# Down-projection of a hybrid decoder layer as seven products of halves, with its weight sums made during attention

## The reference, cut to what matters

```python
hn = rms_norm(h, ffn_norm_w[l])
up = causal_depthwise_conv(hn @ w_up[l], ffn_conv_w[l], ffn_conv_b[l])
a, gt = jnp.split(up, 2, axis=-1)
h = h + (jax.nn.silu(gt) * a) @ w_down[l]
```

## Time and profile before

| | |
|---|---|
| median of 3 runs | 1972.78 us (1972.56 to 1973.24) |
| profiled execution, its own time | 1971.36 us |
| its span | 1969.6 us |
| mean granted TensorE clock | 0.995 of full |
| matmuls | 9113 |
| PE busy | 97% of the span |

### The profile page before, as it was taken

One profiled execution on the slowest core, in us unless ns is written; L12 is line 12 of the kernel. 1 busy time (PEld: TensorE's weight loads), 2 busy tenths in 40 slices (PEclk: granted clock), 3 DMA queues, 4 the chain that ended last, 5 costly groups with the idle time before them and its releaser, 6 DMA issues. The chain is left out here.

```text
span 1969.6 us, 24174 instructions
## 1 busy us (share of the span) xinstructions
PE 1918.9 (97%) x9113; PEld 1646.5 (84%) x9113; DVE 1098.5 (56%) x1413; ACT 738.2 (37%) x1324; POOL 99.1 (5%) x153
## 2 busy tenths in 40 slices
PE   6999999999999998999999999989999999999999
PEld 5788999999998887787888887868888888878887
DVE  5535632453351776897425625478778787643433
ACT  6323532442243154312613322445544454432222
POOL 1101110111010010000100001000000000000000
PEclk9999999999999999999999999999999999999999
DMA  7211221021113101102113405113232232264312
GB/s 245 97 43 44 71 70 43 12 81 49 43 60 113 43 1 43 43 22 65 43 33 93 154 23 171 65 43 97 64 96 74 86 93 67 85 239 146 111 48 75
DMA packets 112412, 152.33 MB, mean 77 GB/s; under 512 B 13705, under 2 KB 60809, under 8 KB 112329
## 3 DMA queue, kind: packets, MB, share of 16 engines
q1 hardware_dynamic: 104265, 140.60, 22.0%
q10 hardware_dynamic: 8064, 10.59, 1.5%
HBM read 122.73 MB, written 28.43 MB: 77 GB/s over the span
## 5 line engine op out<-in xcount | busy, mean ns | idle before, releaser
L240 PE MATMUL psum<-whi,act_lo 128*128 128x512 f32 x768 | 314.9, 410 | 3.5 <-DVE act_lo L1431 2.9
L242 PE MATMUL psum<-whi,act_hi 128*128 128x512 f32 x768 | 304.4, 396 | 0.0
L241 PE MATMUL psum<-wlo,act_hi 128*128 128x512 f32 x768 | 304.4, 396 | 0.0
L240 PEld LDWEIGHTS psum<-whi,act_lo 128*128 128x128 f32 x768 | 194.9, 254 | 18.7 <-issue 4.5
L242 PEld LDWEIGHTS psum<-whi,act_hi 128*128 128x128 f32 x768 | 195.1, 254 | 15.3
L241 PEld LDWEIGHTS psum<-wlo,act_hi 128*128 128x128 f32 x768 | 196.0, 255 | 13.2
L240 PE MATMUL psum<-act_hi,wlo 128*128 128x512 f32 x512 | 202.2, 395 | 1.3 <-DVE wlo L198 1.3
L242 PE MATMUL psum<-act_hi,whi 128*128 128x512 f32 x512 | 199.6, 390 | 0.0
L241 PE MATMUL psum<-act_lo,whi 128*128 128x512 f32 x512 | 199.3, 389 | 0.0
L193 ACT CAST whi<-stage 128x512 fp32r<-128x512 f32 x200 | 120.3, 621 | 180.9 <-PE psum L242 172.6
L198 DVE TENSOR_TENSOR wlo<-stage,whi 128x512 fp32r<-128x512 f32 x200 | 129.0, 686 | 94.7 <-ACT whi L193 93.9
(11 more groups left out here) (248 smaller groups left out, 3572.5 us busy)
## 6 DMA issues: line engine op xcount, KB each, us to landing
stage<-in_w_in SPq DMA_DIRECT2D x144, 256.0 KB, 4.0
u_raw<-in_w_up SPq DMA_DIRECT2D x44, 512.0 KB, 5.0
gated_scratch<-g_buf SPq DMA_DIRECT2D x22, 512.0 KB, 2.7
gated<-gated_scratch SPq DMA_DIRECT2D x22, 512.0 KB, 3.5
d_stage<-in_w_down SPq DMA_DIRECT2D x44, 256.0 KB, 2.8
group_out<-ob ACTq DMA_DIRECT2D x24, 256.0 KB, 2.1
grp<-group_out SPq DMA_DIRECT2D x24, 256.0 KB, 3.2
stage<-in_w_mem_kv SPq DMA_DIRECT2D x16, 256.0 KB, 8.5
```

The costliest lines, as they stand in the source:

```text
L240: nc.tensor.matmul(dst, lhs[1], rhs[0], start=first, stop=False, skip_group_check=True)
L241: nc.tensor.matmul(dst, lhs[0], rhs[1], start=False, stop=False, skip_group_check=True)
L242: return nc.tensor.matmul(dst, lhs[0], rhs[0], start=False, stop=last, skip_group_check=True)
```

## The change

The down-projection becomes seven products of halves. The tokens are cut into two halves (i), the inner dimension into two halves of 11 blocks (j, W_HALF = 11), and the columns into two halves. Each product is one half-by-half product (512 tokens, 1408 inner, 512 columns) of a half, or of a sum of halves, of gated with a half, or a sum of halves, of w_down. Their order is 2, 1, 7, 6, 4, 5, 3. Two sets of four PSUM banks take turns; a product either starts its banks anew or goes on adding to them, and after each product DVE adds the banks to one quadrant of the residual (`add_product`). A "step" is one block of one product: 12 matmuls. There are 77 steps.

- The sums of gated halves are made in place in SBUF (`a_sum`, DVE, 128x512), two steps ahead, for products 7, 6, 5 and 3. Gated tiles are loaded as 44 parts of 128x512.
- The four sums of weight blocks (T1 to T4) are made in the attention stage: for each of 11 block pairs, four raw blocks of w_down are loaded into four slots of `stage` once these are cut, DVE subtracts four times in place in the rounds of tiles 2 and 3 (in two query turns a second group in the rounds of tiles 4 and 5), SP stores the four results to `w_sums` and, when they have landed, loads the weights of the next turn into these slots.
- Weight blocks of the down-projection go through four slots instead of two (raw, high, low, and the high and low half of gated). Three steps are cut inside the last tile of the up-projection. The loops of this stage are written out.
- On SP, the store of gated tile 20 moves behind the first gated loads and block 0, and the store of tile 21 ahead of the gated loads 9 and 10 and of block 4. The residual is loaded by quadrants (1 MB each) at steps 5, 24, 38 and 58, and the output stored by quadrants.

The diff, cut to its core (semaphore offsets and the unchanged parts are left out):

```diff
+        W_SUM_WINDOWS = {}
+        W_SUM_SLOTS = {}
+        for turn in range(BASE_ATT // RING, BASE_ATT // RING + 3 * NG):
+            n = len(W_SUM_SLOTS)
+            W_SUM_WINDOWS[turn] = [n + 1, n] if (turn - BASE_ATT // RING) in (2, 5) else [n]
+            W_SUM_SLOTS[n] = (1, 0) if len(W_SUM_WINDOWS[turn]) == 2 else (0, 4)
+            if len(W_SUM_WINDOWS[turn]) == 2:
+                W_SUM_SLOTS[n + 1] = (0, 4)
...
+        def w_sums_dve(dve, n, which):
+            par, pos0 = W_SUM_SLOTS[n]
+            b11, b12, b21, b22 = (stage[:, pos0 + j, :] for j in range(4))
+            if 0 in which:
+                dve.wait_ge(raw_loaded[par], 64 * w_sums_uses(n))
+            for j in which:
+                if j:
+                    dve.wait_ge(t_sum, 4 * n + j)
+                dst, a, b = ((b11, b12, b11), (b12, b22, b12), (b22, b22, b11), (b21, b21, b22))[j]
+                nc.vector.tensor_tensor(dst, a, b, ALU.subtract).then_inc(t_sum, 1)
...
+                tl = tile_of(part, i, "KVQ")
+                if tl and 2 <= tl.t < 6:
+                    for n in reversed(W_SUM_WINDOWS[tl.turn]) if tl.turn in W_SUM_WINDOWS else ():
+                        order = sorted(W_SUM_WINDOWS[tl.turn]).index(n)
+                        if (tl.t - 2) // 2 == order:
+                            w_sums_dve(dve, n, (0, 1) if tl.t % 2 == 0 else (2, 3))
...
+                def load_blocks(turn, n):
+                    par, pos0 = W_SUM_SLOTS[n]
+                    for j, (k, col) in enumerate(((n, 0), (n, 1), (n + W_HALF, 0), (n + W_HALF, 1))):
+                        pos = pos0 + j
+                        sp.wait_ge(w_lo[pos % 2], 4 * (turn - 1) + pos // 2 + 1)
+                        sp.dma_start(stage[:, pos, :], piece(w_down, k, col * CW)).then_inc(raw_loaded[par], 16)
+                def store_blocks(n):
+                    par, pos0 = W_SUM_SLOTS[n]
+                    sp.wait_ge(t_sum, 4 * (n + 1))
+                    for j in range(4):
+                        sp.dma_start(w_sums[n, j], stage[:, pos0 + j, :]).then_inc(gated_stored[par], 16)
+                def load_turn(turn):
+                    blocks = W_SUM_WINDOWS[turn - 1]
+                    kept = RING - 4 * len(blocks)
+                    for n in blocks[1:]:
+                        load_blocks(turn, n)
+                    for pos in range(kept):
+                        load_slot(sp, turn, pos, sources[turn][pos])
+                    load_blocks(turn, blocks[0])
+                    for n in blocks[1:] + blocks[:1]:
+                        store_blocks(n)
+                    for n in blocks[1:] + blocks[:1]:
+                        par, pos0 = W_SUM_SLOTS[n]
+                        sp.wait_ge(gated_stored[par], w_sums_uses(n) * 64)
+                        for pos in range(pos0, pos0 + 4):
+                            load_slot(sp, turn, pos, sources[turn][pos])
...
+        DOWN_ORDER = (2, 1, 7, 6, 4, 5, 3)
+        DOWN_STEPS = len(DOWN_ORDER) * W_HALF
+        SLOTS = 4
...
+        A_LOADS = [(i, j, k) for i, j in ((1, 2), (1, 1), (2, 1), (2, 2)) for k in range(W_HALF)]
...
+        DOWN_A = {1: (1, 1), 2: (1, 2), 4: (2, 2), 7: (1, 1), 6: (1, 1), 5: (2, 1), 3: (1, 2)}
+        SUM_ORDER = (7, 6, 5, 3)
+        DOWN_B = {1: (0, 0), 2: (1, 0), 3: (1, 1), 4: T4, 5: T1, 6: T2, 7: T3}
...
+        def a_sum(dve, step):
+            p, k = down_step(step)
+            if p not in SUM_ORDER:
+                return
+            if p == 7:
+                a_wait(dve, 2, 1, k)
+                dve.wait_ge(gs_lo_done, DOWN_ORDER.index(1) * W_HALF + k + 1)
+                a, b, op = a_block(1, 1, k), a_block(2, 1, k), ALU.subtract
+            elif p == 6:
+                a_wait(dve, 2, 2, k)
+                dve.wait_ge(gs_lo_done, DOWN_ORDER.index(7) * W_HALF + k + 1)
+                a, b, op = a_block(2, 2, k), a_block(1, 1, k), ALU.subtract
+            elif p == 5:
+                dve.wait_ge(t_sum, sum_count(7, k))
+                a, b, op = a_block(2, 1, k), a_block(2, 2, k), ALU.add
+            else:
+                dve.wait_ge(t_sum, sum_count(6, k))
+                dve.wait_ge(gs_lo_done, DOWN_ORDER.index(2) * W_HALF + k + 1)
+                a, b, op = a_block(1, 2, k), a_block(1, 1, k), ALU.subtract
+            nc.vector.tensor_tensor(a_source(step), a, b, op).then_inc(t_sum, 1)
+        def down_his(act, step):
+            p, k = down_step(step)
+            pos = step % SLOTS
+            if step >= SLOTS:
+                act.wait_ge(w_freed, FREED0 + step - SLOTS + 1)
+            else:
+                act.wait_ge(up_p[(6, 7, 7, 4)[step]], NU)
+            if p in SUM_ORDER:
+                act.wait_ge(t_sum, sum_count(p, k))
+            else:
+                a_wait(act, *DOWN_A[p], k)
+            nc.scalar.copy(a_hi[pos][:], a_source(step)).then_inc(gs_hi_done, 1)
+            act.wait_ge(w_loaded[pos], 16 * (T_DOWN + step // SLOTS + 1))
+            nc.scalar.copy(d_hi[pos][:], d_raw[pos][:]).then_inc(w_hi, 1)
+        def down_lows(dve, step):
+            pos = step % SLOTS
+            dve.wait_ge(gs_hi_done, step + 1)
+            nc.vector.tensor_tensor(a_lo[pos][:], a_source(step), a_hi[pos][:].bitcast(F32),
                                     ALU.subtract).then_inc(gs_lo_done, 1)
-            dve.wait_ge(w_hi, 2 * half_m + (FREED0 + pos + 1))
-            nc.vector.tensor_tensor(d_lo[:, pos, :], d_stage[:, pos, :], d_hi[:, pos, :].bitcast(F32),
-                                    ALU.subtract).then_inc(w_lo[pos], 1)
+            dve.wait_ge(w_hi, HI0 + step + 1)
+            nc.vector.tensor_tensor(d_lo[pos][:], d_raw[pos][:], d_hi[pos][:].bitcast(F32),
+                                    ALU.subtract).then_inc(w_lo[step % 2], 1)
+        FIRST_STEPS = 3
...
-                for U in range(NU - 4, NU - 1):
+                for U in range(NU - 4, NU - 2):
                     up_store(sp, U, U % 2)
...
+                def load_gated(n):
+                    i, j, k = A_LOADS[n]
+                    tile = (j - 1) * W_HALF + k
+                    if n >= 8:
+                        sp.wait_ge(a_loaded[n % 8], 16 * (n // 8 + 1))
+                    sp.wait_ge(gated_stored[tile % 2], GS0[tile % 2] + 16 * (tile // 2 + 1))
+                    sp.dma_start(a_block(i, j, k), gated_dram[tile * P:(tile + 1) * P, (i - 1) * CW:i * CW]
+                                 ).then_inc(a_loaded[n % 8], 16)
...
+                load_gated(0)
                 sp.wait_ge(up_lo[4], NU)
+                for n in range(1, 5):
+                    load_gated(n)
                 sp.wait_ge(up_p[6], NU)
+                load_block(0)
+                for i in (3, 5, 6, 7):
+                    sp.wait_ge(up_lo[i], NU)
+                up_store(sp, NU - 2, 0)
+                sp.wait_ge(up_p[7], NU)
+                load_block(1)
+                load_block(2)
+                load_gated(5)
+                load_gated(6)
                 sp.wait_ge(up_p[4], NU)
+                load_block(3)
+                for n in range(7, 9):
+                    load_gated(n)
+                up_store(sp, NU - 1, 1)
+                for b in h_batches:
+                    sp.wait_ge(h_stored[b], 16 * H_BATCH)
+                for n in range(9, 11):
+                    load_gated(n)
+                for step in range(SLOTS, DOWN_STEPS):
+                    if step + 7 < len(A_LOADS):
+                        load_gated(step + 7)
+                    load_block(step)
+                    if step in RESIDUAL_STEPS:
+                        load_residual(RESIDUAL_STEPS.index(step))
+                    for q, step_q in ((1, 28), (3, 61), (4, 72)):
+                        if step == step_q:
+                            store_quadrant(q)
+                store_quadrant(2)
...
+            RESIDUAL_STEPS = (5, 24, 38, 58)
+            BANKS_E, BANKS_A = (0, 1, 2, 5), (3, 4, 6, 7)
+            PRODUCT = {2: (BANKS_E, True, None, 1), 1: (BANKS_A, True, None, 1), 7: (BANKS_E, True, 0, 4),
+                       6: (BANKS_A, False, 1, 3), 4: (BANKS_E, False, 2, 3), 5: (BANKS_A, False, 3, 4),
+                       3: (BANKS_A, False, 5, 2)}
+            LAST_ADD = {1: 1, 3: 4, 4: 5, 2: 6}
...
+                for n, p in enumerate(DOWN_ORDER):
+                    bank_set, fresh, read, _ = PRODUCT[p]
+                    for k in range(W_HALF):
+                        step = n * W_HALF + k
+                        pos = step % SLOTS
+                        pe.wait_ge(gs_lo_done, step + 1)
+                        pe.wait_ge(w_lo[step % 2], LO0 + step // 2 + 1)
+                        for t in range(4):
+                            if k == 0 and read is not None:
+                                pe.wait_ge(out_ready, 4 * read + t + 1)
+                            if k == 0 and n == 0 and t == 3:
+                                pe.wait_ge(c11_done, NU)
+                            if k == 0 and n == 1 and t < 2:
```

(89 more changed lines are left out.)

167 lines of the change are left out of this document (50 added, 117 removed).

## The result

The changed kernel takes 1951.2 us (median of 4 runs, 1950.67 to 1955.09) where the kernel before takes 1972.67 us: a ratio of 0.9895, interval 0.9878 to 0.9912, or 21.5 us less. The prediction was 1951.5 us.

A forecast was written before the change was run, and what follows sets the result against it. The prediction took PE's number of matmuls to bound the down-projection. Its terms, -29.9 - 2.9 + 3.5 + 4.5 + 2.8 + 0.2 + 0.5 = -21.3 us, gave a forecast of 1951.5 us, range 1944 to 1960.

The forecast's parts named there:

- Fewer matmuls: Down-projection: 924 matmuls instead of 1056, at 0.2267 us each, 29.9 us less.
- Start of the stage: Down-projection start: PE goes on one distance after the up-projection and two old waits go, 2.9 us gained.
- Steady supply: Down-projection's steady part: ACT, DVE and loads keep within 2.72 us a step, so no cost.
- Rival D: Steps 4 to 76: the four-slot block ring bounds the down-projection above 3.07 us a step; 1994 us, chance 0.05.
- The change of banks before product 3: Down-projection: product 3 waits for DVE to add the banks product 5 has just left, 0.2 us.
- The two waits: Down-projection start: PE waits 3.5 us for step 3's lows, then 4.5 us for block 4.
- rule against the change: Tile 21's store: the skill's DMA formula gives 3.2 us, making the second stall 5.0 us and the time 0.5 us longer.
- The clock: After the second stall: TensorE's granted clock falls to half, 2.8 us lost, bounds 0 and 5.6.
- Third stall: Down-projection, step 6, behind the 1 MB residual: no third stall was expected.
- Attention: Attention stage: added sums and moved loads cost one more PE wait, 0.5 us, bounds 0 and 10.
- The 1 us to spare: First double query turn: four late weight loads land by 213.5, ACT reaches slot 4 at about 214.4.
- The sum: Whole kernel: all terms together give -21.3 us, forecast 1951.5 us.

The follow-up runs named there:

- e8: Changed kernel, weight blocks moved ahead of tile 21's store and of gated loads, steps 3 and 4 cut earlier, gated lead shortened, first residual later: 1939.91 us.
- e6: Changed kernel with one more DVE subtraction of 128x512 in each down-projection step from 11 on: 1951.71 us.
- e7: Changed kernel with two more DVE subtractions of 128x512 in each down-projection step from 11 on: 1972.66 us.
- v0_after: The changed kernel again, unedited, run and profiled as reference: 1951.23 us.
- e5: Changed kernel with only the cuts of step 3 moved ahead of the second half of the last up tile's tail: 1952.34 us.
- e3: Changed kernel with loads of weight blocks 4, 5 and 6 moved ahead of the wait for gated tile 21 and its store: 1946.72 us.
- e9: The e3 kernel with the first residual loaded at step 9 instead of 5: 1944.43 us.
- e1: Changed kernel without making or storing block sums in attention; the down-projection takes raw w_down blocks in their place: 1951.57 us.
- e2: Kernel before plus the attention part alone: sums made and stored, never read, old down-projection: 1972.62 us, ratio 1.0004.

## Why the prediction was right, step by step

**Fewer matmuls, 29.9 us.** Shown: in e8 the stage is 924 distances and 0.5 us long.

**Start of the stage, 2.9 us gained.** Right, and 3.6 us by the stages' lengths: the first matmul follows after 0.23 us instead of 1.72 (1.5 us), and the old stage was 241.5 - 1056 x 0.2267 = 2.1 us longer than its matmuls, with its two waits and slow first matmuls. The excess over 2.9 us is the 0.7 us of slow first matmuls, which the prediction had read and not counted as gained.

**Steady supply at nothing.** Right: after step 6 PE never waits in the changed kernel. e6 puts a number on the slack, one more DVE operation of 0.6 us per step, and e7 on its end. Rival D's threshold was 3.07 us a step from 73 steps; in e7, with some 3.2 us in 44 of them (five operations in 3.01 us, and the adds), the time came out level with the kernel before, 21.4 us above the changed one. There DVE is the bound, and not the ring of blocks that rival D named; no run made the loads late in the steady part. The change of banks before product 3, priced at 0.2 us, cost nothing here, but is the first place to give way.

**The two waits, 3.5 and 4.5 us.** They were 4.5 and 3.7 us in one profile, 4.1 and 4.7 us in the other. The places, the engines and the second's cause (a block queued behind a store's landing) are as predicted. That the waits add up to nearly the predicted 8.0 us is chance: what they stand for, the delay of step 4 against four steps without a wait (10.9 us), was 11.1 us (10.9 in v0_after), and step 3 at the low clock filled 2.5 us of it. So this term was 3 us too small, for two reasons. Counted from the stage's first matmul, the tail of the last up tile ended 1.2 us later than computed (0.9 in v0_after), because block 1, which ACT casts ahead of the copy to yg, was there 1.4 us later than I took it (1.1 in v0_after):

```profile
1727.01 0.62 ACT L2226 CAST d_hi<-d_raw 128x512 fp32r<-128x512 f32 x1 [1.80 <-DMA d_raw<-in_w_down]
```

And block 4 landed 5.2 us after its issue (5.3 in v0_after), where I took 3.6; the landing of the store, 2.8 us, was as the row had it (2.7), and not the 3.2 us of the rule against the change. What the Trainium skill states there (DMA: Bandwidth & Descriptors, "Anatomy of one DMA") it states for DMAs issued from GpSimd, and this one is SP's. The same two gated parts, 0.5 MB, stood between the store's landing and the block as I had counted; whether they alone made it late, or also the loads issued behind it, the 1 MB residual among them, no run separates. The two terms are also not two costs: e5 shows that the first wait hides under the second. The start of step 4 is the tail's end plus the way of block 4, and removing the first wait alone gains nothing.

**The clock, 2.8 us.** Right in kind. It fell around the first wait, so that step 3 ran at 1.2 GHz, hidden as I wrote; it rose as step 3 ended and fell again in the second wait, and steps 4 and 5 took 1.6 us too long (2.4 us in v0_after). So this term was too large by 1.2 or 0.4 us. In all 12.8 us were lost where waits and clock had been put at 10.8.

**Third stall: none.** It held in the changed kernel only because steps were late anyway. In e3, where they were not, the residual in front of block 7 cost a wait of 3.1 us and the low clock behind it, which e9 gave back.

**Attention, 0.5 us (0 to 10).** Nothing that can be measured, by e1, e2 and PE's waits. The 1 us to spare that the prediction had left for the late weights was not there, though. In the first double turn ACT began its cuts at 212.90 and took 3.96 us for seven, against 3.75; among all casts of the stage this is the only wait for a load (second line: idle before them, times):

```profile
212.90 3.96 ACT L193 CAST whi<-stage 128x512 fp32r<-128x512 f32 x7
DMA stage<-in_w_in: 0.2, 1
```

The prediction had counted four loads, landed by 213.5; this turn waits for eight. By the trace's semaphore events the last three landed at 215.59, 216.21 and 216.86, and the casts of the first two of them began at 215.61 and 216.24, the moment they were there. It cost PE nothing, but the margin was used up.

**The sum.** -21.3 us predicted, -21.5 measured. From the parts as measured: 29.9 + 3.6 - 12.8 = 20.7, the difference of the stages. The other 0.8 us is no more than medians differ: beside the changed kernel in v0_after the kernel before has 1971.46 us, and the difference is 20.2 us. That the forecast came within 0.2 us is luck: the delay of step 4 was put 3 us too low, the clock 1.2 us too high, the bank change and attention together 0.7 us too high, and the gain at the start 0.7 us too low. The mechanism and each term's sign were right.

## What to carry to other kernels

When an edit saves matmuls, look at the start of its stage: a lead counted in blocks shrinks when blocks get smaller, and what was ready ahead must be counted in microseconds of PE. On one queue in program order a load that waits for a store's landing holds up everything behind it; put what is wanted first ahead of it (e3, e8). And of two waits in a row, take away the one that sets the end: removing the other one gave nothing (e5), removing this one gave 4.5 us (e3).

## What was not expected of the hardware

Waits of nearly the same length had different effects on PE's clock. In e9 a wait of 3.08 us, and in e3 one of 2.98 us, left the granted clock at 1.00; in e3 a wait of 3.14 us, some 14 us later, was followed by 0.50. In the changed kernel it fell 3 us into the wait of 4.49 us, in v0_after 0.4 us after the end of the wait of 4.12 us. A single wait of 3 us is therefore neither safe nor certain to cost anything, and what one cost varied from 0 to about 2.5 us (step 3 took 5.3 us instead of 2.7).

The clock came back once step 3 had run at 0.50: in v0_after at 1739.6, inside the step, in the changed kernel at 1745.7, with its last matmul, and in e1 0.4 us after its end. In the first two it fell again within the wait that followed, before step 4 could use it. In e5, where one wait of 9.8 us stood in place of two, it fell 5.1 us into the wait and stayed at 0.50 for the rest of it and for 5.6 us of matmuls.

```profile
1738.00:1740.00 2.00, 2.00 (x7) 1.49 (x5) 0.00 (x0) 0.00 (x0) 0.00 (x0) 0.60 0.76 235
```
```profile
1740.00:1742.00 2.00, 0.00 (x0) 0.00 (x0) 0.00 (x0) 0.00 (x0) 0.00 (x0) 0.50 0.93 229
```

The first line is v0_after's, with PE busy throughout; the other is e5's, with PE idle.
